# Skewing the stationary and moving blocks of a two-block transformer kernel by 16 bytes in SBUF

## What is computed

```python
for layer in range(2):                       # first block
    h = rms_norm(x, mix_pre_g[layer])
    m = diff_attention(h, a_w_qkv, a_w_o, ...) if layer == 0 else stick_breaking_attention(h, b_w_q, b_w_o, k, v)
    x = x + rms_norm(m, mix_post_g[layer])
    f = swiglu(rms_norm(x, ffn_pre_g[layer]), ffn_w_gate_up[layer], ffn_w_down[layer])
    x = x + rms_norm(f, ffn_post_g[layer])
...
h  = ffn_sublayer(h,  *mods,   g_ffn1, w_ffn1_in, w_ffn1_out)      # second block, latent and context
hc = ffn_sublayer(hc, *mods_c, g_ffn1, w_ffn1_in, w_ffn1_out)
p_lat, p_ctx = project(h, ..., w_in), project(hc, ..., w_in)       # then short conv and mLSTM scans
h = h + mods[5] * merge_branches(...)                              # w_branch_a, w_branch_b, w_out
h = ffn_sublayer(h, *mods, g_ffn2, w_ffn2_in, w_ffn2_out)
return rmsnorm(h, g_final)
```

## Time and profile before

| | |
|---|---|
| median of three runs | 1638.26 us |
| span of the profiled execution | 1637.0 us, 1.3 us below the median |
| PE busy | 1607.3 us, 98% of the span, 10033 matmuls |
| PEld busy (weight loads) | 1406.3 us, 86% |
| DVE, ACT, POOL busy | 1035.9, 826.8, 149.0 us |
| DMA | 309.37 MB, mean 189 GB/s |
| mean granted TensorE clock | full (2.4 GHz) but for two stretches of 3.4 us and the end |

### The profile page before, as it was taken

One profiled execution on the slowest core, in us unless ns is written; L12 is line 12 of the kernel. 1 busy time (PEld: TensorE's weight loads), 2 busy tenths in 40 slices (PEclk: granted clock), 3 DMA queues, 4 the chain that ended last, 5 costly groups with the idle time before them and its releaser, 6 DMA issues.

```text
span 1637.0 us, 24195 instructions
## 1 busy us (share of the span) xinstructions
PE 1607.3 (98%) x10033; PEld 1406.3 (86%) x10033; DVE 1035.9 (63%) x1708; ACT 826.8 (51%) x1191; POOL 149.0 (9%) x141
## 2 busy tenths in 40 slices
PE   7999999999999999999999999999999999999997
PEld 6888888887889988888899999889888888789986
DVE  5686766655645577766665667567747876655554
ACT  4565544443669854444454564444545546354442
POOL 1220010100012200101001100001000000001000
PEclk9999999999999999999999999999999999999999
DMA  9756866777663355555555576598572564575552
GB/s 324 248 192 233 270 211 230 250 249 245 217 207 109 124 190 183 190 196 206 182 179 180 181 157 184 175 196 164 141 153 67 132 171 165 180 250 179 180 191 77
DMA packets 224412, 309.37 MB, mean 189 GB/s; under 512 B 5004, under 2 KB 146720, under 8 KB 224304
## 3 DMA queue, kind: packets, MB, share of 16 engines
q1 hardware_dynamic: 222208, 301.55, 60.2%
q0 software_dynamic: 1664, 5.84, 1.0%
q10 hardware_dynamic: 432, 0.45, 0.1%
HBM read 306.77 MB, written 1.05 MB: 188 GB/s over the span
## 4 chain that ended last, share of the span: by engine, by line
PE 89%; DVE 6%; ACT 3%; issue 1%; DMA 0%; ACTq 0%; DVEq 0%
PE ps L144 86%; PE ps L147 2%; DVE wl L157 2%; DVE SM L167 1%; DVE MT L167 1%; ACT L153 1%; ACT wh L153 1%; ACT SA L153 1%; DVE X L167 0%; ACT FT L153 0%; DVE MT L164 0%; DMA X<-in_x_dram 0%; DVE SM L163 0%; DVE SA L167 0%; ACT YF L153 0%
## 5 line engine op out<-in xcount | busy, mean ns | idle before, releaser
L157 DVE TENSOR_TENSOR wl<-raw,wh 128x1024 fp32r<-128x1024 f32 x498 | 607.8, 1260 | 381.0 <-ACT wh L153 380.3
L144 PE MATMUL ps<-XT,wh 128*128 128x256 f32 (+1 forms) x2880 | 642.2, 311 | 3.0 <-issue 2.2
L153 ACT ACTIVATE wh<-raw 128x1024 fp32r<-128x1024 f32 x498 | 501.5, 1052 | 204.6 <-PE ps L144 114.1
L144 PEld LDWEIGHTS ps<-XT,wh 128*128 128x128 f32 x2880 | 468.2, 189 | 47.3 <-issue 13.6
L144 PE MATMUL ps<-XT,wl 128*128 128x256 f32 x1792 | 502.7, 280 | 0.6 <-DVE wl L157 0.6
L144 PEld LDWEIGHTS ps<-XT,wl 128*128 128x128 f32 x1792 | 337.8, 189 | 1.3 <-DVE wl L157 1.0
L144 PE MATMUL ps<-wh,XT 128*128 128x512 f32 x704 | 224.8, 400 | 0.0
L144 PEld LDWEIGHTS ps<-wh,XT 128*128 128x128 f32 x704 | 131.3, 188 | 32.3 <-issue 1.0
L144 PE MATMUL ps<-wl,XT 128*128 128x512 f32 x352 | 139.0, 395 | 0.0
L144 PE MATMUL ps<-wh,HTH 128*128 128x512 f32 x352 | 137.4, 390 | 0.0
L144 PE MATMUL ps<-wl,HTH 128*128 128x512 f32 x352 | 137.1, 389 | 0.0
(11 more groups left out here) (293 smaller groups left out, 1740.4 us busy)
## 6 DMA issues: line engine op xcount, KB each, us to landing
raw<-in_w_ffn_in_dram SPq DMA_DIRECT2D x66, 1024.0 KB, 5.2
raw<-in_ffn_w_gate_up_dram SPq DMA_DIRECT2D x44, 1024.0 KB, 5.1
raw<-in_w_in_dram SPq DMA_DIRECT2D x40, 1024.0 KB, 8.5
raw<-in_w_ada_dram SPq DMA_DIRECT2D x36, 1024.0 KB, 5.6
raw<-in_w_ffn_out_dram SPq DMA_DIRECT2D x30, 1024.0 KB, 5.0
raw<-in_ffn_w_down_dram SPq DMA_DIRECT2D x20, 1024.0 KB, 5.0
raw<-in_a_w_qkv_dram SPq DMA_DIRECT2D x12, 1024.0 KB, 7.4
raw<-in_kv_w_dram SPq DMA_DIRECT2D x8, 1024.0 KB, 5.5
```

The source lines that it names most:

```text
L144: return NOTHING if self.e is None else self.e.matmul(o, l, r, start=start, stop=stop, skip_group_check=skip)
L153: return self.e.activation(o, i, fn, bias=bias, scale=scale)
L157: return NOTHING if self.e is None else self.e.tensor_tensor(o, a, b, f)
```

## The change

No instruction is added, removed or moved. The tensors' shapes get a margin:

- a block of `XT`, `HTH` and `HTL` takes 260 elements in place of 256, so block k starts 16·k bytes later modulo 64 than before;
- the six slots of `WH` become one tensor with 1028 elements per slot, so slot i starts 16·i bytes later;
- room for this comes from `SM` (small vectors), which shrinks from 248 to 216 columns, its columns for the modulation sums now being those that the spatial gating uses (196 on), and from 32 bytes ahead of `XT` that go.

`XUH`, `XUL`, `HCH`, `HCL` and `WL` keep blocks of 1024 bytes.

```diff
-        WH = [fixed(f"wh{i}", [P, 1024], F32R) for i in range(NHL)]
+        WHS = fixed("wh", [P, NHL, 1028], F32R)
+        WH = [WHS[:, i, 0:1024] for i in range(NHL)]
 ...
-        fixed.o += 32
         xt0 = fixed.o
-        XT = fixed("XT", [P, 2, 8, T], F32R)
+        XT = fixed("XT", [P, 2, 8, T + 4], F32R)[:, :, :, 0:T]
         XTH, XTL = XT[:, 0, :, :], XT[:, 1, :, :]
         C = fixed("C", [P, CK])
-        SM = fixed("SM", [P, 248])
+        SM = fixed("SM", [P, 216])
 ...
-        HTH = f_("HTH", [P, NF, T], F32R)
-        HTL = f_("HTL", [P, NF, T], F32R)
+        HTH = f_("HTH", [P, NF, T + 4], F32R)[:, :, 0:T]
+        HTL = f_("HTL", [P, NF, T + 4], F32R)[:, :, 0:T]
 ...
-        S_MAIN, S_CTX, S_OSS, S_ATT, S_DEN, S_HEAD, S_SGU, S_LAM, S_MOD = 0, 16, 32, 96, 144, 156, 196, 212, 216
+        S_MAIN, S_CTX, S_OSS, S_ATT, S_DEN, S_HEAD, S_SGU, S_LAM, S_MOD = 0, 16, 32, 96, 144, 156, 196, 212, 196
```

## The result

| | before | after |
|---|---|---|
| median, us | 1638.93 (10 runs) | 1643.55 (10 runs, 1642.78 to 1644.88) |
| ratio to before, 95% interval | | 1.0029 [1.0021, 1.0037] |
| span of the profiled execution, us | 1637.0 | 1641.8 |
| PE busy, us | 1607.3 | 1611.2 |

The forecast was 1628 us, faster. The change is 4.6 us slower. The time lies inside my stated range, but on the other side of no change: the sign was wrong. One of the ten runs before took 3232 us; without it their median is 1638.42, and the change costs 5.1 us.

A forecast was written before the change was run, and what follows sets the result against it. PE, busy 1607.3 of 1637.0 us, was taken as the bound through its matmul steps. Terms -3.4 + 3.4 - 0.8 - 5.4 - 1.4 - 2.9 = -10.5 us gave 1626.5, median 1628 us; eight-in-ten range 1597 to 1652.

The forecast's parts named there:

- PE is bound by its own steps, and nothing else moves.: All dense matmuls: spacing of starts sets the time; idle time ahead under 3 us per form, other engines' cost taken as 0.
- What differs is the address of the stationary operand.: 512 columns, weights moving: steps of 227 ns over HTH and HTL but 233 over XUH, put down to the stationary address.
- The distance of their addresses modulo 64 as what tunes it.: All dense forms: distance between moving stream and next weight load, modulo 64 bytes, sets the excess; 227 at 0, 233.4 at 32.
- Distances 16 and 48 are in no row. I put them halfway, at 230.2.: 512 columns: even mix also 230.2 ns; XT -3.4 us, HTH and HTL +3.4, XUH and HCH -0.8.
- 256 columns, -5.4 - 1.4 us, by the 37% carried over from the 512-column form.: 256 columns: distance 0 saves 3.3 ns, an even mix 1.65; -5.4 us over 3264 matmuls, -1.4 over XUH's 832.
- Pairs, -2.9 us.: Paired matmuls, 347 ns a pair: 37% of 22 ns excess, half of it saved, 4.1 ns times 704.
- The excess is the weight load in the stream's way: Dense matmuls: the next weight load reads SBUF beside the moving stream; excess 17.4 ns (XT, 512 columns), 9 ns (256).
- fixed 2: 512 columns: part of a derivation of 216 ns without excess; the prediction text given does not spell it out.
- Rival 1: Distances 16 and 48 are dearer than 32, first over HTH and HTL (+8.4 us); +15.7 us in all, 1654 us; chance 0.25.
- Rival 2: Dense matmuls at distances 16 and 48 have no excess: 1589 us in full, 1614 in half; chance 0.14.
- Rival 3: No effect of addresses, or XT's gains cancel HTH's losses: within 3.3 us of 1638, say 1637; chance 0.19.
- SM, the shared columns, the writes at odd multiples of 16 bytes: nothing.: ScalarE and VectorE, 51% and 63% busy: smaller SM, shared columns and shifted block starts were costed at 0.

The follow-up runs named there:

- hth_128: Kernel before, no margins, with HTH and HTL starting 128 bytes later: 1645.49 us, ratio 1.0038 to the kernel before.
- steps2: Not the transformer: TensorE alone, stretches of 24 matmuls at distances 0 to 496 bytes in steps of 16; 512 columns: 226.7 ns at 0, 232.5 at 128.

## Why the prediction was wrong

- *PE is bound by its own steps, and nothing else moves.* Right. Instruction counts are unchanged, the idle time ahead of each form and the other engines' busy times are so within 1 us; the 4.8 us are all in steps.
- *"What differs is the address of the stationary operand."* Right, and shown: one offset of 128 bytes on HTH and nothing else costs 6 us (hth_128). The rule in the Trainium skill, SBUF — State Buffer, Who interferes with whom, by which PE has two independent read ports and never waits on anyone, does not make addresses free of effect: 5 ns a matmul lie between distances 128 and 256 with nothing else running (steps2).
- *"The distance of their addresses modulo 64 as what tunes it."* Wrong, and the step that failed. The distance counts modulo 256. In the kernel before, XT, XUH and HCH all stood at 160 from WH and HTH at 0, so that the trace showed two values of the distance, and 64, 128 and 256 all fitted them. I took the smallest and filled the places between with straight lines. So I saw neither that every tensor behind a margin would get a new distance by its slide, nor that nearly all of them are as dear as XT's.
- *"Distances 16 and 48 are in no row. I put them halfway, at 230.2."* Wrong. In the row form one distance of sixteen is good, one is fair (64) and the rest are at 231 to 235. There is no slope between 0 and 32; the table's mean is 232.4, the changed kernel's steps 231.6 and 231.8, not 230.2. HTH lost 4.6 ns a matmul and not 3.2, and XT's 512 columns gained 1.6 and not 3.2. ("20.00 us over 85.7" is a slip, 88 less 1.7 being 86.3; the 233.4 itself is right.)
- *256 columns, -5.4 - 1.4 us, by the 37% carried over from the 512-column form.* Wrong. The measured change is -0.5 us (-1.1 over XT, +0.6 over XUH). Distance 0 is among the worst for this form (120.0 ns), not the best; the two forms have different tables.
- *Pairs, -2.9 us.* Wrong in sign: +3.1 (2.8 in their 512 columns, 0.3 in their 256). They stood at 173.3 a matmul, their best, and any mix is above it.
- *The excess is the weight load in the stream's way.* Fell: with 16 columns to load in place of 128 the step is 232 ns. What the excess of 13 ns is, is open; it is per matmul. The "fixed 2" in 2 x 109 less 2 = 216 stands in no row; 384 and 512 columns are 53.4 ns apart in steps2, which makes 213 ns for 512 columns alone.
- *Rival 1*, that HTH loses its good distance, had the right place and the right sign (+8.4 us for HTH, measured +4.8), by a wrong mechanism (odd distances dear). The table's row values at 16 and 48 modulo 64 have a mean of 232.8, those at 32 modulo 64 one of 233.5.
- *Rival 2*, free odd distances: no row value in steps2 at an odd multiple of 16 is below 230 ns. *Rival 3*, a draw: the part by which addresses would not matter is refuted by hth_128; that a skew only trades gains for losses is near to what happened.
- That the time fell into the range of 1597 to 1652 was luck: the range was wide for rivals whose mechanisms did not occur.
- *SM, the shared columns, the writes at odd multiples of 16 bytes: nothing.* Right so far as the trace can tell.

## What to carry to other kernels

In a kernel whose fp32r matmuls run back to back, the base addresses of stationary and moving tensors relative to each other are a tuning knob (0.75% here) that costs nothing, and it has to be measured for each form of matmul. A stretch of 24 matmuls per distance on TensorE alone gives the whole table in one run. For 512 columns the kernels came within 0.7 ns of it, but for XT at 144 and 192 (1 to 2 ns above); for 256 columns it was off by up to 5 ns, so a choice has to be tried in the kernel. A margin that slides later tensors changes their distances too, and can cost more than the margin brings: compare the distances of all tensors, modulo 256, before and after. A skew gave about the table's average; where a good constant distance exists, it is better to keep to it.

## What was unexpected of the hardware

- The mean steps of a stretch of fp32r matmuls are multiples of 6.67 ns at about half of the distances: 113.3 and 120.0 for 256 columns, 226.7 and 233.3 for 512, 173.3 for 384.
- The distance counts modulo 256 bytes, and down to 4 bytes: 226.7 ns at 0, 236.7 at 4.
- Between two distances that alternate with every matmul, 0 (226.7) and 32 (233.3), the step is 235.0 ns, above both. Why is open.
- A stretch of 256-column matmuls at one and the same distance settled at 113 ns in one run and at 119 in another. What decides it is open.
